# Token-tile by token-tile norms, turns and router products, written-out expert pairs, and earlier first loads in a two-layer hybrid MoE step

## The reference, cut to what matters

```python
for layer in range(DEPTH):
    hs = _modulate(xs, norm1_g[layer], ms[0], ms[1])      # rmsnorm * (1 + scale) + shift
    ys = mixer(hs)                                        # recurrent (0) or attention (1), ends in @ w_out
    xs = xs + ms[2][:, None, :] * ys
    xs = xs + ms[5][:, None, :] * _expert_choice_moe(_modulate(xs, norm2_g[layer], ms[3], ms[4]), *moe)
    # and the same for the context tokens xp with their own modulation mp

def _expert_choice_moe(xn, w_router, w_gate, w_up, w_down):
    aff = softmax(xt @ w_router)
    g, idx = lax.top_k(aff.T, cap)
    xe = xt[idx]
    h = silu(xe @ w_gate) * (xe @ w_up)
    ye = (h @ w_down) * g[..., None]
    return zeros.at[idx].add(ye)
```

## Time and profile before

| | us |
|---|---|
| median of 3 runs (lowest, highest) | 1890.08 (1889.51, 1894.63) |
| profiled execution, its time | 1888.88 |
| its span | 1886.9 |
| PE busy | 1660.1 (88%) |
| DVE, ACT, POOL busy | 602.3, 364.8, 312.2 |
| DMA mean | 278 GB/s, 525.07 MB |

### The profile page before, as it was taken

One profiled execution on the slowest core, in us unless ns is written; L12 is line 12 of the kernel. 1 busy time (PEld: TensorE's weight loads), 2 busy tenths in 40 slices (PEclk: granted clock), 3 DMA queues, 4 the chain that ended last, 5 costly groups with the idle time before them and its releaser, 6 DMA issues.

```text
span 1886.9 us, 30470 instructions
## 1 busy us (share of the span) xinstructions
PE 1660.1 (88%) x13255; PEld 771.5 (41%) x13255; DVE 602.3 (32%) x1077; ACT 364.8 (19%) x725; POOL 312.2 (17%) x358
## 2 busy tenths in 40 slices
PE   4799868479999999999989788893899999999997
PEld 0688546123332322332258666562233233233322
DVE  2568564510110110120176577535101101210102
ACT  2377731100000000000052365402000000000000
POOL 1133230110101110110020167301101101101110
PEclk8899979789999999999989899896899999999999
DMA  9400642989999999999830201019799999999993
GB/s 391 139 1 1 246 167 112 414 328 407 379 409 375 392 406 371 385 406 413 333 137 1 95 24 33 36 44 417 268 395 391 405 366 388 407 373 391 411 358 116
DMA packets 57682, 525.07 MB, mean 278 GB/s; under 512 B 12351, under 2 KB 12639, under 8 KB 24782
## 3 DMA queue, kind: packets, MB, share of 16 engines
q1 hardware_dynamic: 47968, 490.62, 64.5%
q0 software_dynamic: 8176, 27.08, 5.3%
q10 hardware_dynamic: 1406, 5.38, 0.7%
HBM read 500.50 MB, written 22.55 MB: 277 GB/s over the span
## 4 chain that ended last, share of the span: by engine, by line
PE 77%; DVE 10%; DMA 5%; ACT 4%; issue 3%; POOL 1%; SPq 0%; DVEq 0%; POOLq 0%; ACTq 0%
PE ps L862 36%; PE ps L866 17%; PE ps L813 6%; PE ps L1104 4%; DMA W<-x_hat,gi_c 2%; DMA ring<-in_mod_w 2%; DMA ring<-in_rg_w_in 1%; PE ps L1152 1%; PE ps L1139 1%; PE ps L1126 1%; PE ps L889 1%; PE ps L1024 1%; PE ps L904 1%; ACT W L1332 1%; PE ps L1002 1%
## 5 line engine op out<-in xcount | busy, mean ns | idle before, releaser
L862 PE MATMUL ps<-ring,W 128*32 128x512 f32 x4608 | 558.4, 603 | 19.3 <-issue 18.0
L866 PE MATMUL ps<-ring,W 128*16 128x512 f32 x2304 | 300.6, 594 | 0.0
L862 PEld LDWEIGHTS ps<-ring,W 128*32 128x32 f32 x4608 | 146.8, 111 | 353.3 <-issue 351.1
L1172 ACT ACTIVATE W<-ps 128x512 f32<-128x512 f32 (+5 forms) x129 | 70.3, 562 | 923.1 <-PE ps L904 730.4
L1621 DVE TENSOR_TENSOR W<-ps,amod 128x1024 f32<-128x1024 f32 (+1 forms) x32 | 28.5, 891 | 516.1 <-PE ps L889 394.7
L862 PE MATMUL ps<-over_rows,W 128*32 128x512 f32 x1536 | 182.7, 593 | 0.0
L866 PEld LDWEIGHTS ps<-ring,W 128*16 128x16 f32 x2304 | 68.2, 98 | 179.7 <-issue 179.7
L1630 DVE TENSOR_TENSOR W<-ps,W 128x1024 f32<-128x1024 f32 x16 | 19.6, 1224 | 278.1 <-PE ps L866 278.1
L813 PE MATMUL ps<-wo_hl,mo_hi 128*128 128x512 f32 x320 | 89.2, 402 | 14.6 <-DVE mo_lo L1541 14.6
L866 PE MATMUL ps<-over_rows,W 128*16 128x512 f32 x768 | 100.0, 592 | 0.0
L862 PEld LDWEIGHTS ps<-over_rows,W 128*32 128x32 f32 x1536 | 48.4, 110 | 108.0 <-issue 107.6
(11 more groups left out here) (277 smaller groups left out, 2172.2 us busy)
## 6 DMA issues: line engine op xcount, KB each, us to landing
ring<-in_moe_w_down SPq DMA_DIRECT2D x52, 2048.0 KB, 11.5
ring<-in_moe_w_up SPq DMA_DIRECT2D x48, 2048.0 KB, 13.0
ring<-in_moe_w_gate SPq DMA_DIRECT2D x44, 2048.0 KB, 9.8
ring<-in_mod_w SPq DMA_DIRECT2D x48, 1024.0 KB, 10.7
over_rows<-in_moe_w_gate SPq DMA_DIRECT2D x20, 2048.0 KB, 11.3
over_rows<-in_moe_w_up SPq DMA_DIRECT2D x16, 2048.0 KB, 9.3
over_rows<-in_moe_w_down SPq DMA_DIRECT2D x12, 2048.0 KB, 12.7
ring<-in_rg_w_in SPq DMA_DIRECT2D x8, 1024.0 KB, 27.4
```

Of the source, the lines that this page charges most:

```text
L862: nc.tensor.matmul(ps[q * CG:(q + 1) * CG, bank + n, :], lat(q, k), expert_slots(slots[q // 2], 1)[:, 0, cols], start=(k == 0), stop=(k == ...
L866: mm = nc.tensor.matmul(ps[q * CG:q * CG + CC, bank + 2, :], ctx(a, k), expert_slots(slots[a], 1)[:, 0, h * D + n * 512:h * D + (n + 1) * ...
L1172: nc.scalar.activation(out, in_, ACT.Copy).then_inc(done, n)
```

## The change

Six edits are made together; names and memory places change with them.

1. After a mixer's tile t is produced and gated, its norm is made at once (sum of squares now always on DVE in phases 1 and 3), PE turns it after tile t+1 (`turn_rows`), multiplies with the router after tile t+2 and adds the partial sums after tile t+3. `last_logits` holds what is left after the fifth tile. Evictions of turned tiles are 128 x 128, four on ACT and four on DVE a tile.
2. x and its normalised copy are stored in five DMAs each, tile by tile. The normalised tiles live in two buffers in W, so the row buffers need no store of all of them to have landed; in layer 1 they wait for the first gather instead.
3. PE's eight pairs of experts are written out; the other engines keep their loops.
4. Between the layers the norms and turns go by tiles behind the one-hot sums: the turns of the first two tiles lie inside `last_rows`, the others behind `modulation(10)`. A tile's turn waits for the evictions of the one before it (one pair of banks, 5 and 7).
5. `modulation(11)` moves from behind the attention's output product into the end of the attention loop, so that SP can load the first experts of layer 1 (n = 8, 10) during the output product.
6. The copy of the recurrent state's last row goes before the output product.

```diff
@@ SP
+            def store_x(layer, x1, tiles):
+                for t in tiles:
+                    sp.wait_ge(x1_ok, 2 * (NT * layer + t + 1))
+                    sp.dma_start(x_res[layer][t * P:(t + 1) * P, :], tok(x1)[:, t, :]).then_inc(x1_stored, 16)
...
-                    sp.wait_ge(x1_stored, 16 * (layer + 1))
-                    sp.wait_ge(xh_stored, 16 * (layer + 1))
-                    sp.wait_ge(tr_mm, 4 * KB * (layer + 1))
+                    sp.wait_ge(x1_stored, 16 * NT * (layer + 1))
+                    sp.wait_ge(out_mm, NT * (layer + 1))
+                    sp.wait_ge(xhat_ok, 2 * NT * (layer + 1))
...
+                    store_x(1, r2, range(TL))
                     sp.wait_ge(out_mm, 2 * NT)
                     for n in range(16, 24, 2):
                         first(n)
+                    store_x(1, r2, range(TL, NT))
+                    sp.wait_ge(gathered, 32 * NP + 32)
                     row_buffers()
...
             load_mod(5, wo_lo_ok, lambda s: 2 * (s + 1))
+            store_x(0, r1, range(TL))
             for v in (6, 7):
                 load_mod(v, out_mm, lambda s: NT)
-            store_x(0, r1)
+            store_x(0, r1, range(TL, NT))
@@ PE
+            def turn_rows(phase, t, xh, banks):
+                n = row_at(phase, t)
+                pe.wait_ge(xhat_ok, NT * phase + t + 1)
+                if t:
+                    pe.wait_ge(row_act, n)
+                    pe.wait_ge(row_dve, n)
+                for b in range(KB):
+                    mm = nc.tensor.transpose(ps[:, banks[b // 4], (b % 4) * P:(b % 4 + 1) * P], xh[:, b * P:(b + 1) * P], ident[:, :])
+                mm.then_inc(row_mm, 1)
+            def last_logits(layer):
+                logit_parts(layer, 3)
+                logit_sums(layer, 2)
+                turn_rows(2 * layer + 1, TL, xh_tile[TL % 2], (4, 5))
+                logit_sums(layer, 3)
+                logit_parts(layer, 4)
+                logit_sums(layer, 4)
@@ PE, mixer_out, behind each tile
-                    if t == 0 and after_first is not None:
+                    if t == 0:
                         after_first()
+                    else:
+                        if t == 1:
+                            pe.wait_ge(gate_ok, 4 * (layer + 1))
+                        turn_rows(2 * layer + 1, t - 1, xh_tile[(t - 1) % 2], (4, 5))
+                    if t >= 2:
+                        logit_parts(layer, t - 2)
+                    if t >= 3:
+                        logit_sums(layer, t - 3)
@@ PE, experts
-                steps(pe, body)
+                for i in range(NP):
+                    body(i, i % 2, i < NP - 1, i < NP - 2)
@@ PE, between the layers
-            last_rows(0)
+            def between_rows(t):
+                if t >= 3:
+                    turn_x(t - 3)
+            last_rows(0, between_rows)
             modulation(10, turn_last=False)
-            pe.wait_ge(mod_read, 10)
-            turn(2)
+            for t in range(2, NT):
+                turn_x(t)
@@ PE, attention loop
+                if i == NU + 1:
+                    pe.wait_ge(s_max, 2 * NU)
+                    modulation(11, turn_last=False)
+            pe.wait_ge(mod_row, 12)
             pe.wait_ge(o_ok, NU)
             mixer_out(1, lambda: gate_rows(1, diag1))
-            pe.wait_ge(gate_ok, 8)
-            modulation(11, turn_last=False)
-            turn(3, 1)
+            last_logits(1)
@@ ACT, between the layers
-            squares(2, 0, x2_ok, first_weights)
+            for t in range(NT + 3):
+                if t < NT:
+                    square(t)
+                if 1 <= t <= NT:
+                    row_root(2, t - 1)
+                if t in (2, 4):
+                    qkv_high(QKV_ORDER[t // 2 - 1])
+                if t >= 3:
+                    rows_turned(2, 1, t - 3, feat(r1)[:, :, (t - 3) * P:(t - 2) * P], 5)
             mod_reads([10], turn_last=False)
             for k in QKV_ORDER[2:4]:
                 qkv_high(k)
-            turned(2, 1)
@@ ACT, behind the attention loop
+            mod_reads([11], turn_last=False)
             mixed_high(1)
             gate_copy(1, gb1)
-            squares(3, 2 * NT)
-            mod_reads([11], turn_last=False)
-            store_xhat(1)
-            turned(3, 1)
-            logit_sums(1)
+            normed(1)
@@ DVE, residual, each tile
+                    v.tensor_tensor_reduce(out=xh, in0=x[:, t, :], in1=x[:, t, :], scale=1.0, scalar=0.0,
+                                           op0=ALU.mult, op1=ALU.add, accum_out=sm[:, phase, 0, t:t + 1]).then_inc(row_sq, 1)
+                    row_var_of(phase, t)
+                    if t >= 1:
+                        logits(layer, t - 1)
+                    row_scale(phase, t, x[:, t, :], xh)
+                logits(layer, TL)
```

More of the change, by code:

```diff
@@ L227, in build @@
         ob_c = work(D)
-        parts = ob_l[:, 0:NTOK]
+        xh_tile = [W[:, 7168 + u * D:7168 + (u + 1) * D] for u in range(2)]
+        xt_tile = [W[:, 11776 + u * D:11776 + (u + 1) * D].rearrange("p (k n) -> p k n", k=KB) for u in range(2)]
+        parts = [W[:, 9344 + u * P:9344 + (u + 1) * P] for u in range(2)]
         merge = W[:, 14592 - NE:]
@@ L585, in experts @@
                 pool.wait_ge(route_ok, 10 * (layer + 1))
-                pool.wait_ge(xh_stored, 16 * (layer + 1))
-                pool.wait_ge(x1_stored, 16 * (layer + 1))
+                for u in range(2):
+                    pool.wait_ge(xh_stored[u], 16 * xh_stores(u) * (layer + 1))
+                pool.wait_ge(x1_stored, 16 * NT * (layer + 1))
                 pool.wait_ge(stored, 16)
@@ new lines, in logit_parts @@
+            def logit_parts(layer, t):
+                n = row_at(2 * layer + 1, t)
+                pe.wait_ge(row_act, n + 1)
+                pe.wait_ge(row_dve, n + 1)
+                if t:
+                    pe.wait_ge(part_ok, NT * layer + t)
+                else:
+                    pe.wait_ge(router_in, 32)
+                    pe.wait_ge(pad_ok, 1)
+                for g in range(2):
+                    for q in range(4):
+                        k = 4 * g + q
+                        at = (layer * KB + k) * NE
+                        mm = nc.tensor.matmul(ps[q * CG:(q + 1) * CG, 6, 0:P], router_all[:, at:at + CG], xt_tile[t % 2][:, k, :],
+                                              start=(g == 0), stop=(g == 1))
+                mm.then_inc(part_mm, 1)
@@ new lines, in logit_sums @@
+            def logit_sums(layer, t):
+                pe.wait_ge(merge_ok, 3 * (layer + 1))
+                pe.wait_ge(part_ok, NT * layer + t + 1)
+                mm = nc.tensor.matmul(ps[:, 7, t * NE:(t + 1) * NE], parts[t % 2], merge[:, :], start=True, stop=True)
+                mm.then_inc(merge_mm, 1)
+            def last_logits(layer):
[5 more added lines that the diff above has]
+                logit_sums(layer, 4)
@@ L967, in last_rows @@
                     mm.then_inc(add_mm, 1)
+                    if after is not None:
+                        after(t)
             pe.wait_ge(consts, 1)
@@ new lines, in logits, with parts_out, normed @@
+            def logits(layer, t):
+                phase = 2 * layer + 1
+                if t >= 2:
+                    act.wait_ge(part_mm, NT * layer + t - 1)
+                rows_turned(phase, layer, t, xt_tile[t % 2], 4)
+            def parts_out(layer, t):
+                act.wait_ge(part_mm, NT * layer + t + 1)
+                if t >= 2:
+                    act.wait_ge(merge_mm, NT * layer + t - 1)
+                copy(parts[t % 2], ps[:, 6, 0:P], part_ok)
+            def normed(layer, after_last=None):
+                phase = 2 * layer + 1
+                for t in range(NT):
+                    if t >= 1:
+                        logits(layer, t - 1)
+                    if t >= 2:
+                        parts_out(layer, t - 2)
+                    row_root(phase, t)
+                    act.wait_ge(xhat_ok, NT * phase + t + 1)
+                    act.dma_start(x_hat[layer][t * P:(t + 1) * P, :], xh_tile[t % 2]).then_inc(xh_stored[t % 2], 16)
+                if after_last is not None:
+                    after_last()
+                parts_out(layer, 3)
+                logits(layer, 4)
+                parts_out(layer, 4)
@@ L1244, in gate_copy @@
                         copy(out[:, s, n * 512:(n + 1) * 512], ps[:, 4 + 2 * s + n, :], gate_ok)
-            def logit_sums(layer):
-                act.wait_ge(part_mm, layer + 1)
-                copy(parts[:, 0:NLAT], ps[:, 4, :], part_ok)
             def softmax(layer):
@@ L1503, in norm_end, with norm_inputs @@
                 norm_scale(phase, 1)
-            def turned(phase, layer, between=None):
+            def norm_inputs(phase, layer):
                 eng.wait_ge(mod_ok, NMOD * layer + 3 * (phase % 2) + 2)
@@ L1666, in experts, with last_rows @@
                 steps(eng, body)
-            def last_rows(layer):
```

(1 more changed line is left out.)

202 lines of the change are left out of this document (100 added, 102 removed).

## The result

| | us |
|---|---|
| before, median of 4 runs on the same chip (lowest, highest) | 1892.36 (1889.51, 1896.25) |
| after, median of 4 runs | 1865.77 (1864.07, 1867.68) |
| ratio after/before, 95% interval | 0.9865 [0.9847, 0.9884] |
| profiled execution before, after | 1888.88, 1864.11 |
| span before, after | 1886.9, 1862.3 |

The kernel is faster by 1.35%; predicted were 1862 us and a range of 1847 to 1876. A later group of runs of both kernels has a ratio of 0.9889 [0.9872, 0.9906]: by the medians the gain is 26.6 us in the first group and 20.7 in the later one.

The account below looks back on a forecast made before the run. PE, busy 1660.1 of 1886.9 us, was taken as the bound, gains being its idle or lower-clock time. Terms -22.6 - 4.1 - 4 - 4.6 + 7 = -28.3 took the median 1890.08 to 1861.8, said as 1862; range 1847 to 1876.

Parts of the forecast that it names:

- Written-out pairs, -22.6: Expert stages: removes four jumps on PE at 5.64 us each, -22.6 us; -15 if only the pauses go.
- the picture of the reserve: Expert weight loads: without jumps landing time grows to some 24 us, still under the 38 until a slot is needed.
- Layer 0 to softmax, -4.1: Layer 0, output product to router: 16.4 us against 20.5, so -4.1; bounds 0 and -6.
- softmax 16 us behind the fifth tile: Layer 0, sign that the steps are right: softmax begins 16 us after the fifth tile.
- Second gather of layer 0, -4: Layer 0: queue ends some 5 us earlier, so the 14.11 us gather gains between 0 and -9.6; taken -4.
- The row beside attention: Layer 1, modulation(11) in attention: +4 us, bounds +1 and +7, with up to -2.4 credited for a higher clock.
- Between the layers, +7: Experts' end to first query product: query input +6.2 us later, +8.7 at PE's lower clock; bounds +3 and +10, taken +7.
- the sign's 5 to 9: Between the layers: first query product 5 to 9 us later after the first add, 28.5 before.
- B: Rival, gathers run free: both meet short queues and PE stays warm, 12.6 us more gain, 1849 us; chance 0.18.
- C: Rival, loads become the bound: landing passes 38 us, about half the loop gain lost, 1873 us; chance 0.12.
- D: Rival, written-out code starves PE: instruction-fetch pauses come with code, 1941 us if one in each pair; chance 0.03.
- E: Rival: only the pauses go (-15) and every other part costs its upper bound; +0.4 us, no change; chance 0.03.

Follow-up runs that it names:

- held loads: Changed kernel, layer 0: loads of the third product's slots (four of 2 MB) issued only when the second pair's gathers have landed; 1859.03 us, ratio 0.9836.
- before again: The kernel before, unchanged, run once more for a second trace; 1889.95 us.
- the last kernel: Changed kernel with third-product loads held, row-buffer loads moved, between-layers step shortened and its waits filled with query input and weight parts; 1829.58 us, ratio 0.9693.
- gathers free: Changed kernel with shortened between-layers step, third-product loads held in layer 0 and row-buffer loads moved in both layers; 1843.17 us, ratio 0.9751.
- both: Changed kernel with layer 0's third-product loads held until the second gathers landed, and the step between the layers shortened; 1850.20 us, ratio 0.9789.
- loops only: The kernel before with one thing of the change: PE's expert pairs written out, no loop; 1872.78 us, ratio 0.9903.

## Why the prediction was right

The time was right within 4 us, and most terms with it. That the sum came out so close is in part luck: three misses one way (second gather 3.1 us, the row 1.4, and 2.7 in attention that was in no term) met two the other way (2.2 between the layers, 1.4 before softmax 0). Against the 20.7 us of the later group, -28.3 is 7.6 too much. By steps:

**Written-out pairs, -22.6.** The two expert stages shrank by 11.7 and 10.3, 22.0. Putting the loops back cost 24.5 there, some 21.7 without the spell at the low clock. The pause of 3.8 us and the stretch at the lower clock behind it were rightly taken as one price. What was wrong is the picture of the reserve: landing was to grow to some 24 us and stayed at 12.8. A load is issued when a slot comes free, so with PE at a constant pace I read a constant time as natural, and the growth in the earlier trace rows as what follows a jump.

**Layer 0 to softmax, -4.1.** Measured -5.5: 4.3 us until the fifth tile (4.7 said) and 10.7 behind it (11.7 said). The sign "softmax 16 us behind the fifth tile" contradicts that working: 16.4 counts from where the tile was ready before.

**Second gather of layer 0, -4: the step that failed.** It gained 1.0. I had the stores in pieces shorten the queue, by some 5 us, with routing 4.1 earlier. These two numbers leave the gather 0.9 us; the -4 was a choice between the bounds that the working did not give. The last of the four loads of 2 MB that both kernels issue beside the gathers, at 366.8 us before and at 361.4 after, took

```profile
DMA to landing us min/median/max: 31.3/31.3/31.3
...
DMA to landing us min/median/max: 29.7/29.7/29.7
```

to land. So the queue did end 7.0 us earlier, but the gather was issued 6.0 earlier (378.18 against 384.21), and in both kernels it lands as the last of these loads does, with DMA at a share of 1.01 up to there (345 to 391.4 us in the changed kernel). The stores set when the queue ends, not how much of it stands beside the gather. Holding those loads showed it: 7.1 us at once.

**Layer 1.** The row beside attention was taken at +4 and cost 5.4 (with against without, 153.3 and 147.9): at the lower clock it ran 5.47 us, and the following output tile was no faster, 12.8 us. The credit of up to 2.4 us for a warmer PE that I let in did not come. Routing -3, measured -3.6; first gather -8.6, measured -8.5; second +3, measured +3.7. That 4.5 us of the -8.5 hang on the row's early slots was not seen in the prediction, which put all of it on the row-buffer loads.

**Between the layers, +7.** Measured +4.8. The turns stayed at the higher clock (1.04 to 1.09 each), so the warm value +6.2 is the one to compare; the tile cycle was 2.77 us, not 3.0, and ACT began the query input 28.0 us behind the first add, not 29.5. The first query product came 33.3 us behind the first add, 4.7 later than before and just short of the sign's 5 to 9. The Trainium skill (TensorE: Matmul & The Clock Gate, HAM oscillation) gives as its rule to leave PE no long idle gaps. The gaps before these turns were at most 1.80 us in the changed kernel, where they stayed at the higher clock; they were no longer in the trace with held loads, where two of the same five turns took 1.94 us. So that rule does not decide this place.

**Not in the sum:** 2.7 us more in attention, with nothing changed in it.

Sum of the stages: -0.9 -5.5 +0.3 -0.9 -11.7 +4.8 -0.4 +8.0 -3.6 -8.4 +3.7 -10.3 = -24.9, where I had -28.3; the span fell by 24.6, since the 14 us behind the last boundary grew by some 0.4. The rivals: B fell, since neither gather of layer 0 met a short queue; C and D fell with landing times of 12.8 us and a chain without "issue"; E with the total.

What the study adds: by the stages, 22.0 us of the gain are those of the written-out pairs. The rest of the change wins 5.5 and 3.6 us before the softmaxes and 9.5 at two gathers, and pays 4.8 between the layers, 5.4 in attention and 3.7 at the last gather: some 4.7 us net, of which the clock takes 2.7 in attention. In whole executions that is hardly seen: with the loops in place the rest has a ratio of 1.0009, and with the pairs written out it is the step from 0.9903, the pairs alone, to 0.9865 or 0.9889, the whole change.

## What to carry to other kernels

- An engine's loop whose body is all that the chain consists of pays its jump each time: compare the distance of the same instruction inside a pass and over the jump, not only the pause.
- A step cut into tiles wins only where the engines have the waits to put the pieces in. List what each engine does behind the last piece; whatever does not depend on it belongs into the waits ahead. Here that, and one more pair of banks, turned +4.8 us into -3.
- A small transfer on the critical path is delayed by loads nobody needs for another 30 us. Hold those by a wait on its landing; the reserve to watch is their landing time against the time until the slot is needed.

## What the hardware did that I had not expected

The clock differs between kernels in stretches that are the same code. In some of them it repeats in a second trace of the same kernel, in others it does not. In attention, 24 us behind the last query product, rows of before again, after and the last kernel (columns as in the earlier trace rows):

```profile
1083.70:1089.70 6.00, 5.07 (x54) 4.04 (x54) 3.95 (x18) 3.87 (x14) 2.93 (x2) 1.00 0.00 0
```

```profile
1069.58:1075.58 6.00, 6.00 (x48) 4.77 (x50) 2.93 (x13) 2.94 (x10) 2.04 (x2) 0.72 0.00 0
```

```profile
1042.02:1048.02 6.00, 5.06 (x54) 4.04 (x55) 3.98 (x17) 3.88 (x14) 2.94 (x2) 1.00 0.00 0
```

Granted clock 1.00, 0.72 and 1.00, with no DMA in any. The spell comes twice, 24 us apart, in ten of the twelve kernels profiled, not in before and not in the last (1.00 is full speed, 2.4 GHz; 0.50, at 1.2 GHz, the other level; 0.72 is a mean over both). It costs 2.7 to 3.0 us (attention 145.2 in before; 147.9 and 148.2 in the two other kernels without the row there). The last pair of experts has the same: its last 30 us in the changed kernel, with gathers free, and with all of it,

```profile
884.10:914.10 30.00, 26.76 (x248) 8.40 (x244) 2.40 (x4) 1.62 (x2) 3.13 (x5) 1.00 0.86 316
```

```profile
870.80:900.80 30.00, 26.76 (x224) 7.86 (x220) 2.40 (x4) 1.62 (x2) 2.12 (x4) 0.89 0.92 351
```

```profile
866.10:896.10 30.00, 26.76 (x248) 8.40 (x244) 2.41 (x4) 1.62 (x2) 3.92 (x5) 1.00 0.93 370
```

with the same 3.24 us of waits in each (30.00 less PE's 26.76). In the trace of the kernel with all edits none of these spells happens: that, and not only its edits, is why it came out 20.6 us under "both". Comparing it with "gathers free", 2.8 us lie in attention and 2.7 and 3.0 in the two expert stages, 8.5 us of its 15.1. Spells of this kind are also part of why the loops are worth 16.5 us of span in one order and 26.2 in the other: in "loops only" the last 30 us of the experts of layer 1 ran at 0.89.

This end of layer 1's experts also differs between two executions of one kernel. The first and the second trace of the changed kernel:

```profile
1817.60:1847.60 30.00, 25.30 (x232) 7.83 (x224) 3.79 (x6) 1.62 (x2) 1.24 (x3) 1.00 0.24 88
```

```profile
1818.00:1848.00 30.00, 25.39 (x216) 7.64 (x208) 3.70 (x6) 1.62 (x2) 1.24 (x3) 0.94 0.24 88
```

Before has 1.00 and 0.94 there too, and its last stage is 1.5 us longer in the second trace. Whole executions show the same: of the last kernel's five, four took 1828.61 to 1829.95 us at a mean granted clock of 0.960 to 0.962, and one took 1837.13 at 0.955. Of the 35 of before beside the three groups, all below 1890 us had 0.946 to 0.950, the three slowest (1894.56 to 1897.82) 0.939 to 0.944.

What sets the clock down in one kernel and not in another, with the same work before it, stays open; the start time of the stretch differs between all of them, but no run here varied that alone. On this kernel a difference of up to some 8 us between two versions may thus be the clock's. An edit is better judged by its own stage.
